# An expert FFN's down-weight loads moved from SyncE's DMA queue to ScalarE's

## What is computed

```python
gates, idx = lax.top_k(affinity.transpose(0, 2, 1), cap)       # 16 experts, 64 tokens each
xin = h[bidx, idx]
hid = silu(einsum('becd,edf->becf', xin, w_gate)) * einsum('becd,edf->becf', xin, w_up)
y = einsum('becf,efd->becd', hid, w_down) * gates[..., None]   # d = 1024, f = 2048
return zeros_like(h).at[bidx, idx].add(y)
```

## Time and profile before

| what | value |
|---|---|
| median of 3 runs | 2849.86 us (2847.04 to 2849.97) |
| the profiled execution's own time | 2849.99 us |
| its span in the trace | 2848.0 us |
| TensorE busy | 2691.0 us, 94% of the span |
| DMA queues | 558.34 MB, mean 196 GB/s |
| VectorE, ScalarE, GpSimd busy | 33%, 24%, 8% |

### The profile page before, as it was taken

How to read it: one execution, slowest core, us unless ns; L and a number is a source line. 1 busy time by engine, 2 the same in 40 slices (tenths; PEclk the granted TensorE clock), 3 DMA queues, 4 the chain that set the end, 5 groups by cost and what they waited for, 6 DMA issues and landing times.

```text
span 2848.0 us, 36716 instructions
## 1 busy us (share of the span) xinstructions
PE 2691.0 (94%) x15767; PEld 1910.0 (67%) x15767; DVE 941.0 (33%) x1520; ACT 671.3 (24%) x1149; POOL 229.3 (8%) x235
## 2 busy tenths in 40 slices
PE   7999799999999999999899999999999988999998
PEld 4755664444444444444688689999988876788886
DVE  4656531111211112111533434332243143533323
ACT  3327320000100101000321423212232133321222
POOL 2434010000000000000203300000000060000000
PEclk9999799999999999999899899999999999999998
DMA  7280049999999999999221112233232011223321
GB/s 270 102 308 28 30 159 379 428 428 429 428 429 428 428 429 428 429 428 415 57 66 38 45 45 75 75 107 94 70 87 76 23 60 30 74 80 106 95 82 52
DMA packets 238671, 558.34 MB, mean 196 GB/s; under 512 B 29689, under 2 KB 191875, under 8 KB 213596
## 3 DMA queue, kind: packets, MB, share of 16 engines
q1 hardware_dynamic: 234160, 548.48, 50.1%
q0 software_dynamic: 1488, 5.70, 0.6%
q10 hardware_dynamic: 2908, 2.47, 0.3%
HBM read 552.40 MB, written 4.23 MB: 195 GB/s over the span
## 4 chain that ended last, share of the span: by engine, by line
PE 78%; DMA 8%; DVE 5%; ACT 3%; issue 1%; POOL 0%; DVEq 0%; ACTq 0%
PE vpsum L2272 21%; PE apsum L2272 11%; PE vpsum L2134 10%; PE vpsum L2151 9%; DMA ring<-w_down 8%; PE apsum L2117 4%; PE apsum L2281 3%; PE apsum L2298 2%; PE vpsum L2298 2%; PE apsum L2183 1%; PE vpsum L2183 1%; PE apsum L2202 1%; PE vpsum L1874 1%; PE apsum L2364 1%; PE vpsum L1865 1%
## 5 line engine op out<-in xcount | busy, mean ns | idle before, releaser
L2134 PE MATMUL vpsum<-ring,arena 128*64 128x512 f32 x2048 | 444.7, 595 | 0.9 <-DVE arena L1546 0.9
L2272 PE MATMUL vpsum<-work_r,wring_r 128*128 128x264 f32 (+1 forms) x2160 | 346.1, 322 | 3.3 <-DVE work_r L1724 3.3
L2134 PEld LDWEIGHTS vpsum<-ring,arena 128*64 128x64 f32 x2048 | 146.4, 137 | 290.7 <-issue 290.7
L2272 PEld LDWEIGHTS vpsum<-work_r,wring_r 128*128 128x128 f32 x2160 | 312.1, 189 | 37.5 <-issue 5.9
L2272 PE MATMUL apsum<-stream_r,wring_r 128*128 128x264 f32 (+1 forms) x2208 | 334.0, 311 | 0.0
L2272 PEld LDWEIGHTS apsum<-stream_r,wring_r 128*128 128x128 f32 x2208 | 306.1, 191 | 22.0 <-issue 1.1
L1629 DVE TENSOR_TENSOR wring_r<-wring,wring_r 128x2048 fp32r<-128x2048 f32 (+2 forms) x97 | 200.3, 2069 | 349.8 <-ACT wring_r L1070 349.8
L2272 PE MATMUL vpsum<-stream_r,wring_r 128*128 128x264 f32 (+1 forms) x1728 | 273.5, 317 | 10.5 <-DVE body L1712 10.5
L1070 ACT ACTIVATE wring_r<-wring 128x2048 fp32r<-128x2048 f32 (+3 forms) x100 | 172.6, 1728 | 469.6 <-DMA wring<-w_ffn 449.6
L2272 PEld LDWEIGHTS vpsum<-stream_r,wring_r 128*128 128x128 f32 x1728 | 246.8, 191 | 31.8 <-DVE body L1712 10.9
L2151 PE MATMUL vpsum<-ring,arena 128*64 128x512 f32 x1024 | 244.6, 633 | 23.3 <-DMA ring<-w_down 23.1
(11 more groups left out here) (445 smaller groups left out, 3033.8 us busy)
## 6 DMA issues: line engine op xcount, KB each, us to landing
ring<-w_gate SPq DMA_DIRECT2D x64, 2048.0 KB, 20.5
ring<-w_up SPq DMA_DIRECT2D x64, 2048.0 KB, 14.4
ring<-w_down SPq DMA_DIRECT2D x64, 2048.0 KB, 18.5
wring<-w_ffn SPq DMA_DIRECT2D x88, 512.0 KB, 4.7
ring<-w_ada SPq DMA_DIRECT2D x12, 2048.0 KB, 15.0
wring<-w_ffn SPq DMA_DIRECT2D x32, 704.0 KB, 4.4
ring<-w_in SPq DMA_DIRECT2D x5, 2048.0 KB, 16.4
wring<-w_in SPq DMA_DIRECT2D x10, 1024.0 KB, 5.6
```

The source lines that it names most:

```text
L2134: last = pe.matmul(banks[g][CAP * blk:CAP * blk + CAP, :], xin[:, 2 * r + c, :], w[:, at:at + 512], start=r + c == 0, stop=r + c == 4)
L2272: last = pe.matmul(dst, w_[:, c, col:col + P], x_.bitcast(FR), start=c == 0 and i == 0, stop=c == chunks - 1 and i == 2)
```

## The change

ScalarE issues the four down-weight loads j8 to j11 of each expert at the head of its expert loop, with the same waits and into the same slots with the same semaphores; SP issues j6 and j7 and then j0' to j5'. Nothing else differs.

```diff
-        def expert_unit(sp, e, j):
+        def expert_unit(queue, e, j):
...
-                sp.lower_val(offset * 4)
+                queue.lower_val(offset * 4)
...
             with sp.Fori(0, NE - 1) as e:
-                load_expert(e, range(6, 12))
+                load_expert(e, range(6, 8))
                 load_expert(e + 1, range(6))
-            load_expert(NE - 1, range(6, 12))
+            load_expert(NE - 1, range(6, 8))
...
             with act.Fori(0, NE) as e:
+                for j in range(8, 12):
+                    src = expert_unit(act, e, j)
+                    act.wait_ge(gu_done, 8 * e + j - 6 + 1)
+                    act.dma_start(expert_slot(j), src).then_inc(loaded[(MOE_U + j) % NSLOT], 16)
                 for g in range(2):
                     act.wait_ge(gu_done, 8 * e + 4)
```

## The result

The changed kernel takes 2884.0 us (median of 4 runs, 2879.24 to 2887.89) against 2849.91 us: a ratio of 1.012, 95% interval 1.0097 to 1.0142. It is **34 us slower**; 10 were forecast. The profiled execution took 2879.24 us (span 2877.5), 29.3 more than before. One execution in all that follows is left out of the times, the profiled one of the kernel in which ScalarE issues only j10 and j11: it took 9195 us, with the matmuls of L2155 at 1918 ns on average where 660 is usual, while ScalarE's and VectorE's instructions took as long as ever.

What follows compares the result with a forecast made beforehand. Expert loads through the DMA engines were taken to set the pace, with TensorE having 2.8 us to spare per expert. Terms 4.8 + 5.6 = +10.4 on 2849.99 gave 2860.4 us; range 2845 to 2890.

Steps and rivals of the forecast that it cites:

- Bound and place: Expert loop, 457 to 1341 us: loads set the pace, 58.7 us per expert against TensorE's 55.9; DMA engines must stay fed.
- Issue cost and ScalarE's waits: Expert loop: four issues moved from SP to ScalarE gain and lose nothing; 4.2 us of cover remain before VectorE wants SiLU's result.
- Order of transfer: Expert loop: j0' and j1' run beside j10 and j11, so j11 lands 9 us later and becomes the awaited load.
- Halves: Assumed sharing of the DMA engines between the two queues: some 18 us shared, 9 of them to SP's j0' and j1'.
- Term 1, the end of the loop: After the last awaited load: the loop's last down product ends at F + 13.2 instead of F + 8.4, +4.8 us.
- Term 2, the reserve: Behind j11 only 10.6 us of loads remain; a fallen clock in a third of 14 experts idles engines 1.2 us each, +5.6 us.
- the case's own 2854 to 2880: Range in us given for the forecast's main case alone, around 2860.4 us; its chance was 0.54.
- The order was not kept: Rival: hardware drains both queues in order of issue, j11 ahead of j0', so nothing moves, 2850 us; chance 0.15.
- No queue was preferred: Rival: SP's queue is served more, j10 and j11 wait behind j0' to j3'; +140 at the limit, 2990 us; chance 0.10.
- Two queues moved less and not more: Rival: engines alternating between two streams hide seams between packets and move more, 2840 us; chance 0.06.
- Turns of whole loads: Rival: queues alternate load by load, waits of 5.6 us before `down(e, 1)` in every second expert; +18, 2868 us; chance 0.15.

## Why the prediction was right, and what in it was too small

*Bound and place.* Right. The loads set the pace, TensorE needed 55.9 of 58.7 us, and everything hung on whether the engines stay full.

*Issue cost and ScalarE's waits.* Right: 0.34 us for each issue, no wait of L1560 for ScalarE, and no cost with all twelve on ScalarE.

*Order of transfer.* Right in kind. The waits moved to j11, 15 of 2.8 us where some 14 of 2.8 were forecast; w_gate landed after 15.4 instead of 20.5 us. I had w_down landing later than 18.5 at the median; it was 14.7, since j8 and j9 now land sooner (12.2 and 13.7 us in the expert at 599 us) and j11 late (25.7). Halves were right for the shared stretch; that a load lands only with its last packets, up to 5.0 us after the 16th from its end, was not in the prediction.

*Term 1, the end of the loop, +4.8 us.* Failed: it measured -0.8. Before, the last load landed at 1328.9 + 21.7 = 1350.6 us and the last product ended 11.2 us later, where the prediction has 8.4: it put the product behind the last wait at 7.0 us, although that product took 9.66. After, the last load landed at 1364.5 + 17.0 = 1381.5 and the last product ended at 1391.9, 10.4 later, where the prediction has 13.2: j11 of expert 14 landed 54.3 us ahead of the last load and not 49.7, and the product behind it took 8.8 us. The landing itself moved by 30.9 us, which is term 2.

*Term 2, the reserve, +5.6 us.* The mechanism was right and this is the term that was mis-sized: it measured 31. Four things were short in it. The product behind the wait was slowed in 14 experts of 15 and not in a third (what that alone cost the runs leave open). The reserve behind j11 was smaller than 10.6 us in the longest waits, since j11's last packets came late while SP's queue moved on: dry after 8 us in the expert shown. I followed the engines only to the issue of j4'; behind it comes a second gap before j6', about half of the idle. And slow packets, mostly the first after an engine had run dry, are 14 of the 32 us. My upper bound of +24 for this term therefore was no bound; the measured 34 us lies inside the stated range of 2845 to 2890 but outside the case's own 2854 to 2880. That the stated range holds it is in part luck: its top comes from the forecast's and the whole-load bounds, and neither has the second gap or the slow packets in it.

*Rivals.* The order was not kept. No queue was preferred, and the loss is far from 140 us. Two queues moved less and not more. Turns of whole loads, at +18, come out nearer to the time than my forecast, and one sign of theirs was seen: the first eight waits are 4.1, 1.5, 5.4, 1.4, 6.5, 1.5, 4.0 and 1.5 us, long and short by turns. Their mechanism was not: in the packet records of the shared stretches the two queues' 16 KB packets take turns one by one. The Trainium skill's page "DMA: Bandwidth & Descriptors", section "Queues, rings and completion order", has engines switch between queues packet by packet; that agrees, with a packet here being a row of 16 KB. Its sentence that starting DMAs on several engines saves only issue time, section "Issuing engines are not separate DMA queues", held as to gain; that it can cost 1.2% is what this case adds.

## What to carry to other kernels

Where loads go round a ring of slots and set the pace, ask what the DMA engines still have to do when the load that is waited for lands, and how long until the next issue; that reserve, not the mean rate, decides. A second queue makes loads land out of the order of use, and each one that lands early holds a slot without being work, so it thins the reserve even though every load waits for the same counts as before. A load also lands only with its last packets, and those can lag. If issues must be spread over engines, keep on one queue whatever follows the awaited load, as the kernel with j0' and j1' behind j11 did at no cost, and follow a gap further than its first issue.

## What was not expected of the hardware

A 16 KB packet took 0.61 us in a steady stream and 1.06 us on average where it started with fewer than 15 under way; all slow packets together were 14 us of the 32 lost. Two busy queues were served in equal turns of one packet, 50 to 51% for either stream. But a 2 MB load was held up by its last packets: the time from its 16th packet from the end to its last went from 0.8 to 5.0 us, and the other queue moved up to 115 packets meanwhile.
